# Other tables for the filling of the attention units, and sums of parts ahead of the low parts

## The reference, cut to what matters

```
proj = rmsnorm(x) @ w_in            # q_d k_d v_d  q_n k_n v_n  gate_b gate_c h_in
y_dil = dilated_attention(rope(q_d), rope(k_d), v_d)
y_na  = neighbourhood_attention(q_n, k_n, v_n, rpb)
y_conv = gate_b * conv3(gate_c * h_in)
x = x + rmsnorm(concat(y_dil, y_na, y_conv) @ w_out)
x = x + rmsnorm((silu(hf @ w_gate) * (hf @ w_up)) @ w_down)
```

## Time and profile before

| | us |
|---|---|
| median of 3 runs | 3051.28 |
| lowest, highest | 3050.6, 3051.84 |
| the profiled execution | 3046.58 |
| its span, first to last instruction | 3044.7 |
| TensorE busy in it | 2987.1 |
| VectorE busy | 2002.5 |
| ScalarE busy | 1242.8 |
| GpSimd busy | 937.6 |
| granted TensorE clock, mean | 0.998 |

### The profile page before, as it was taken

One profiled execution on the slowest core, in us unless ns is written; L12 is line 12 of the kernel. 1 busy time (PEld: TensorE's weight loads), 2 busy tenths in 40 slices (PEclk: granted clock), 3 DMA queues, 4 the chain that ended last, 5 costly groups with the idle time before them and its releaser, 6 DMA issues.

```text
span 3044.7 us, 50957 instructions
## 1 busy us (share of the span) xinstructions
PE 2987.1 (98%) x19620; PEld 2817.0 (93%) x19620; DVE 2002.5 (66%) x3740; ACT 1242.8 (41%) x2405; POOL 937.6 (31%) x757
## 2 busy tenths in 40 slices
PE   9999999999999999999999999999999999999997
PEld 7888877899999999999988888879999999999997
DVE  6766756388744447677877666563887444486787
ACT  5433444544422224444554334344544222254342
POOL 1211111664542225101542112117656222260011
PEclk9999999999999999999999999999999999999999
DMA  4111011333322115544521110113332221257345
GB/s 155 44 58 52 22 39 42 109 110 104 110 68 68 68 68 195 203 146 153 186 102 44 51 55 15 46 49 115 104 110 93 85 72 68 70 182 252 98 141 193
DMA packets 151519, 300.31 MB, mean 99 GB/s; under 512 B 16240, under 2 KB 74224, under 8 KB 151024
## 3 DMA queue, kind: packets, MB, share of 16 engines
q1 hardware_dynamic: 148976, 289.18, 28.5%
q10 hardware_dynamic: 2304, 7.87, 0.6%
HBM read 231.45 MB, written 57.67 MB: 95 GB/s over the span
## 4 chain that ended last, share of the span: by engine, by line
PE 87%; DVE 6%; issue 2%; POOL 1%; ACT 1%; DMA 1%; SPq 0%; POOLq 0%; DVEq 0%; ACTq 0%
PE PS L2606 26%; PE PS L2608 25%; PE PS L2607 25%; PE PS L2758 4%; PE PS L2727 4%; PE PS L2742 3%; PE PS L2644 1%; DVE PT L2334 1%; POOL OSS L1205 1%; DVE ACCUM L1938 1%; PE PS L2702 0%; ACT PT L1531 0%; DMA EYE<-small 0%; DVE ACCUM L1936 0%; DVE YB L2321 0%
## 5 line engine op out<-in xcount | busy, mean ns | idle before, releaser
L2606 PE MATMUL PS<-XH,WH 128*128 128x512 f32 (+1 forms) x1152 | 432.3, 375 | 14.6 <-DVE Rv L2208 4.1
L2608 PE MATMUL PS<-XH,WL 128*128 128x512 f32 (+1 forms) x1152 | 409.4, 355 | 0.0
L2607 PE MATMUL PS<-XL,WH 128*128 128x512 f32 (+1 forms) x1152 | 408.1, 354 | 0.0
L1227 POOL TENSOR_TENSOR GL<-GR,GH 128x512 fp32r<-128x512 f32 x186 | 252.1, 1367 | 366.4 <-ACT GH L1574 299.9
L2606 PE MATMUL PS<-DHH,DWH 128*128 128x384 f32 (+1 forms) x1056 | 328.5, 311 | 0.6 <-DVE ACCUM L2168 0.6
L2608 PE MATMUL PS<-DHH,DWL 128*128 128x384 f32 (+1 forms) x1056 | 326.6, 309 | 0.0
L2607 PE MATMUL PS<-DHL,DWH 128*128 128x384 f32 (+1 forms) x1056 | 325.8, 309 | 0.0
L2606 PEld LDWEIGHTS PS<-XH,WH 128*128 128x128 f32 x1152 | 217.0, 188 | 71.3 <-issue 19.6
L2334 DVE TENSOR_TENSOR PT<-PS,PT 128x512 fp32r<-128x512 f32 (+1 forms) x328 | 165.6, 538 | 165.3 <-ACT PT L1531 162.7
L2608 PEld LDWEIGHTS PS<-XH,WL 128*128 128x128 f32 x1152 | 217.1, 188 | 32.7
L1531 ACT ACTIVATE PT<-PS 128x512 fp32r<-128x512 f32 (+1 forms) x328 | 142.9, 477 | 247.2 <-PE PS L2742 242.8
(11 more groups left out here) (243 smaller groups left out, 8318.1 us busy)
## 6 DMA issues: line engine op xcount, KB each, us to landing
GR<-w_gu SPq DMA_DIRECT2D x62, 768.0 KB, 4.1
RAW<-w_in SPq DMA_DIRECT2D x48, 512.0 KB, 3.4
DHR<-hidden SPq DMA_DIRECT2D x66, 320.0 KB, 4.4
DWR<-w_down SPq DMA_DIRECT2D x66, 256.0 KB, 3.9
S3B<-w_down SPq DMA_DIRECT2D x66, 256.0 KB, 3.1
GR<-w_gu SPq DMA_DIRECT2D x62, 256.0 KB, 2.5
T3B<-hidden SPq DMA_DIRECT2D x44, 320.0 KB, 3.8
hidden<-S1T SPq DMA_DIRECT2D x44, 192.0 KB, 1.9
```

Of the source, the lines that this page charges most:

```text
L1227: nc.gpsimd.tensor_tensor(GL[v % 2][:, m, :, :], GR[v % 2][:, m, :, :], GH[v % 2][:, m, :, :].bitcast(F32), ALU.subtract).then_inc(s_wlo_r ...
L2606: nc.tensor.matmul(out, wh, xh, start=first, stop=False, skip_group_check=reopened)
L2607: nc.tensor.matmul(out, wh, xl, start=False, stop=False, skip_group_check=reopened)
L2608: return nc.tensor.matmul(out, wl, xh, start=False, stop=last, skip_group_check=reopened)
```

## The change

- `FILL_TILES` replaces `FILL_WIDTH`: the number of tiles of each step is written out. In blocks 0 and 1 a group still takes 4 + 4 tiles, the short one all 8 in one unit; in blocks 2 and 3 the nine groups take 19 units (the first group 2, 3, 3; the short one of k and q 2, 6); in block 4 the six groups take all 20 units.
- `SHORT_FIRST`: in four of the column tiles the short chunk is made first: order 2, 0, 1. With 4 + 4, 4 + 4 and 8 this sets at which units groups end.
- `ROPE_AT`: ropes stand in a table by unit, instead of one unit behind the group.
- SyncE's swaps follow the new order, and the load of ("q", 2) moves ahead of the last swap of ("q", 1).
- Taps: units 3, 5, 7 instead of 0, 1, 2 in block 2; 7, 8, 9 instead of 9, 10, 11 in block 4. GpSimd's scalings follow.
- `add_parts` stands ahead of the low parts of its unit instead of behind.
- At the start of block 4 the three bias operations stand behind the first drain and the split of v.

```diff
-FILL_FROM = (0, 0, 1, 1, 1)
-FILL_WIDTH = ((2, 2, 1) * 4, (2, 2, 1) * 4, (2,) * 9, (2,) * 9, (3,) * 6)
+FILL_FROM = (0, 0, 1, 1, 0)
+SHORT_FIRST = {("k", 1), ("v", 1), ("q", 2), ("c", 1)}
+EVEN, LATE, WHOLE, SLOW = (4, 4), (2, 6), (8,), (2, 3, 3)
...
+              ((2, 3, 3), (3, 1, 4), LATE, (1, 3, 1, 3), (1, 3, 1, 3), (2, 2, 2, 2)))
+ROPE_AT = ({7: ("k", 1, 2), 9: ("k", 1, 0), 11: ("k", 1, 1), 13: ("q", 1, 0), 15: ("q", 1, 1), 17: ("q", 1, 2)},
+           {3: ("k", 2, 0), 5: ("k", 2, 1), 6: ("k", 2, 2), 8: ("q", 2, 2), 9: ("q", 2, 0), 11: ("q", 2, 1)}, {}, {}, {})
+def chunks_in_turn(unit):
+    return (2, 0, 1) if unit in SHORT_FIRST else (0, 1, 2)
+def last_chunk(unit):
+    return chunks_in_turn(unit)[-1]
 def fill_steps(L, b):
     steps = [(None, 0, 0)] * FILL_FROM[b]
-    for group, width in zip(fill_groups(L, b), FILL_WIDTH[b]):
-        cuts = [KT * n // width for n in range(width + 1)]
-        steps += [(group, cuts[n], cuts[n + 1]) for n in range(width)]
+    for group, counts in zip(fill_groups(L, b), FILL_TILES[b]):
+        assert sum(counts) == KT
+        steps += [(group, sum(counts[:n]), sum(counts[:n + 1])) for n in range(len(counts))]
...
                 load((L, "k", 2))
-                for c in range(NCH):
+                for c in range(2):
                     swap(L, "q", 1, c)
                 load((L, "q", 2))
+                swap(L, "q", 1, 2)
...
-                        if (b, u) in ((0, 7), (2, 2), (4, 11)):
+                        if (b, u) in ((0, 7), (2, 7), (4, 9)):
                             scale_taps(L, b // 2)
...
                         y(u // 2 - 1)
+                    if u and u % 2 == 0:
+                        add_parts(u // 2 - 1)
                     for g, (a, n) in enumerate(quads(units[u][3])):
...
-                    if u and u % 2 == 0:
-                        add_parts(u // 2 - 1)
...
+                    drain(*cover[0])
+                    split_v(nb, slice(0, 4))
                     if b == LAST:
                         masked_biases(L, 1, 0)
                         masked_biases(L, 1, 1)
                         inner_biases(L, 1)
-                    drain(*cover[0])
-                    split_v(nb, slice(0, 4))
...
-                        if u and steps[u - 1][2] == KT and steps[u - 1][0] in ROPE:
-                            rope(*steps[u - 1][0])
+                        if u in ROPE_AT[b]:
+                            rope(L, *ROPE_AT[b][u])
...
-                        if b == 2 and u < 3:
-                            tap(L, 1, u)
+                        if b == 2 and u in (3, 5, 7):
+                            tap(L, 1, u // 2 - 1)
...
-                        if b == LAST and 9 <= u < 12:
-                            tap(L, 2, u - 9)
+                        if b == LAST and 7 <= u < 10:
+                            tap(L, 2, u - 7)
```

More of the change, by code:

```diff
@@ L168 @@
         (("h", 2), ("b", 2)))
-FILL_FROM = (0, 0, 1, 1, 1)
-FILL_WIDTH = ((2, 2, 1) * 4, (2, 2, 1) * 4, (2,) * 9, (2,) * 9, (3,) * 6)
+FILL_FROM = (0, 0, 1, 1, 0)
+SHORT_FIRST = {("k", 1), ("v", 1), ("q", 2), ("c", 1)}
+EVEN, LATE, WHOLE, SLOW = (4, 4), (2, 6), (8,), (2, 3, 3)
+FILL_TILES = ((EVEN, EVEN, WHOLE, WHOLE, EVEN, EVEN) * 2, (EVEN, EVEN, WHOLE, WHOLE, EVEN, EVEN) * 2,
+              (SLOW, EVEN, LATE, EVEN, EVEN, LATE, EVEN, EVEN, EVEN), (SLOW, EVEN, LATE, EVEN, EVEN, LATE, EVEN, EVEN, EVEN),
+              ((2, 3, 3), (3, 1, 4), LATE, (1, 3, 1, 3), (1, 3, 1, 3), (2, 2, 2, 2)))
[5 more added lines that the diff above has]
+    return chunks_in_turn(unit)[-1]
 def fill_groups(L, b):
-    return [(L, kind, i, c) for kind, i in FILL[b] for c in range(NCH)]
+    return [(L, kind, i, c) for kind, i in FILL[b] for c in chunks_in_turn((kind, i))]
 def cover_groups(L, b):
@@ L689, in final @@
             L, kind, i = unit
-            return GROUP[unit + (NOC - 1 if kind == "o" else 2,)]
+            return GROUP[unit + (NOC - 1 if kind == "o" else last_chunk((kind, i)),)]
         def gcol(L, which, k):
@@ L1038, in biases @@
                 if j == 0:
-                    sp.wait_ge(s_rope, ROPE[L, "q", 2, 2])
+                    sp.wait_ge(s_rope, ROPE[L, "q", 2, last_chunk(("q", 2))])
                     sp.dma_start(CMASK[:, :], tables[:, 2 * T + NLOG:]).then_inc(s_bias_in, 16)
@@ L1072, in _ @@
                 load((L, "b", 0))
-                for c in range(NCH):
+                for c in chunks_in_turn(("k", 1)):
                     swap(L, "k", 1, c)
                 load((L, "k", 2))
-                for c in range(NCH):
+                for c in range(2):
                     swap(L, "q", 1, c)
                 load((L, "q", 2))
+                swap(L, "q", 1, 2)
                 load((L, "v", 2))
@@ L1085, in _ @@
                 load((L, "h", 1))
-                for c in range(NCH):
+                for c in chunks_in_turn(("q", 2)):
                     swap(L, "q", 2, c)
@@ L2781, in fill @@
                     tiles(key, range(t0, t1))
-                drained((L, "v", b, 2))
+                drained((L, "v", b, last_chunk(("v", b))))
                 turn_v(nb, slice(0, 4))
```

## The result

The changed kernel takes 3019.07 us (median of four runs, 3017.97 to 3020.45), the kernel before 3051.56 beside it: a ratio of 0.9892, 95% interval 0.9881 to 0.9904. That is 32.5 us faster; 25.4 was forecast. A second series of the changed kernel gave 3019.43 (0.9894, 0.9875 to 0.9912).

The account below looks back on a forecast made before the run. TensorE, busy 2987.1 of 3044.7 us, was taken as the bound; only its attention stops could go. Per layer 22.2 falls to 2.0 + 2.6 + 2.8 + 2.1 = 9.5, 25.4 for two layers: 3026 us, range 3015 to 3040.

Parts of the forecast that it names:

- The ceiling of 22.2: TensorE's stops in a layer's attention blocks, 14.0 us idle plus about 0.2 for each of some 45: the most to win.
- A: Fill steps that open a group and wait for the last group's drain: 25 places, 10.5 us a layer falling to 2.0.
- B: Values that wait for the low parts of odd units: 12 places, 7.1 us a layer falling to 2.6.
- C: Transposes, `spread_recip` and one scores that wait for VectorE: 9 places, 4.6 us a layer falling to 2.8.
- The ports: Moved ropes and a tap on VectorE meet GpSimd's low parts of weights at shared SBUF ports: 2.1 us a layer lost.
- At no cost: Block 4's biases behind the first drain (scores' wait about 0.3, in C) and q's earlier load, said to move no wait.
- The sums: `add_parts` ahead of low parts: `spread_recip` loses its wait, low parts come 0 to 0.4 us later; counted in C.
- Rival 1: The ports take it back: five meetings a layer cost 2.0 us each instead of 0.4, giving 3042; chance 0.15.
- Rival 3: Stops only move: the gain of A comes back in B and C, giving 3047 us; chance 0.07.
- Rival 4: Slower: sums hold up low parts, 0.83 us for each pair that pays; at 45 pairs 3063 us; chance 0.03.
- rival 2: More goes than counted: block 4's stops (4.7 a layer after) halve, ports cost nothing, 9 us more, 3017; chance 0.15.
- The signs: Checks: idle 14.0 to about 6 us, few drain waits, stretches 11 to 14 shorter, nothing outside moving over a microsecond.

Follow-up runs that it names:

- blocks01_back: The changed kernel with blocks 0 and 1 as before (old tables, chunk order and rope places), the sums still ahead: 3028.39 us, ratio 0.9916.
- lows_apart: The changed kernel with GpSimd's low parts of weights kept out of VectorE's ropes and taps by waits: layer 0's blocks 475.65 us, against 476.30.
- both sums kernels: The kernel before with only the sums moved ahead of the low parts, 3046.2 us; the changed kernel with the sums behind them again, 3032.78 us.
- ropes_later: The changed kernel with every rope of blocks 0 and 1 one unit later, tables and drains unchanged: 3042.21 us in one run.

## Where the prediction was right and where not

The time lies in the range, and the stops that went are those of the text; the gain was forecast 3.5 us a layer too small (12.7 against 16.2). Several terms were taken too large and one stop of 1.0 wasn't seen, and these misses partly cancel: that the miss isn't larger is luck. Step by step, start against start in the timeline of layer 0 of the changed kernel:

- **The ceiling of 22.2.** What is left after is about 7.3 a layer where 9.5 was forecast, so the counted stops fell by 14.9. The blocks gained 16.3: the other 1.4 are gaps of 0.1 and less behind each stop, that weren't counted. So 22.2 was no ceiling, but 1.4 or more below it.
- **A, 10.5 to 2.0.** Right. Unit 18 of blocks 0 to 3 keeps 0.34 each, exactly the estimate from the drain's length; unit 3 of block 4 has 0.58 for 0.45, and the short groups behind one another cost 0.06 where no port meeting falls on them. It is 2.0 in all, beside 0.4 that goes to the ports.
- **B, 7.1 to 2.6.** It is 1.8 without the ports and the load. The value that was most off is unit 9 of block 4, taken at 1.3: 0.74. TensorE and VectorE there:

```profile
526.37 0.39 PE L2625 MATMUL PS<-XH,WL 128*128 128x512 f32 x1
527.34 1.43 PE L2775 MATMUL PS<-PT,V 128*128 128x256 f32 x10 [0.58 <-DVE PT L2353]
```

```profile
524.21 1.54 DVE L2271 SCALAR_TENSOR_TENSOR TA<-TC,STAT,TA 128x1281 f32<-128x1281 f32 x1
525.67 0.60 DVE L2338 TENSOR_TENSOR YB<-PS,YS 64x128 f32<-64x128 f32 x2
526.31 0.89 DVE L2353 TENSOR_TENSOR PT<-PS,PT 128x512 fp32r<-128x512 f32 x2
```

  The order of tap, outputs and low parts is as forecast and ends at 527.20. But the tap starts already 0.21 behind the unit's transposes (524.00), and three tiles of fill keep TensorE until 526.6; I had let the tap start later. The forecast set out from the 0.74 that this order cost before, and left out that the sums ahead free VectorE for the tap: with the sums ahead alone, that stop (unit 11 there) is 0.23.
- **C, 4.6 to 2.8.** It is 1.9. Counted up to the next transposes, units 10, 12, 14, 16 and 18 of block 4 wait 0.14, nothing, 0.24, 0.15 and 0.91, for the 0.5, 0.1, 0.45, 0.35 and 1.0 forecast. (The 2.63 of the earlier trace rows holds for unit 16 alone; in unit 18 the two transposes were 2.51 apart.) Block 4 in all was the largest miss: 4.7 forecast, 3.25 found, and its length fell by 3.2 where 1.2 was forecast.
- **The ports, 2.1.** The meetings at the units 11 came as forecast and cost nothing instead of 0.55 each; a late rope at the end of an odd unit has the slack, since nobody waits for its product soon. The one in unit 3 of block 1 makes the drain two units on late (0.4, for 0.1 forecast), that of the tap in unit 6 of block 0 makes the values behind it late (0.2, for 0.4), and the one in unit 6 of block 1 (0.5) didn't take place: together 0.6 a layer. "SBUF — State Buffer" of the Trainium skill, section "SBUF: two separate sides", speaks of a lock held for a whole instruction; the 2.52 beside 2.38 agree, and so does the drain from PSUM that keeps its length. The rule says how long VectorE is blocked, not whether TensorE waits for what VectorE does next: that is where the prediction was 1.5 off.
- **At no cost.** Here a step failed. The queue of SyncE was looked at for q only; the load of `h` 1 behind a swap of `k` 2 waits for a moved rope, and costs 1.0. It is why block 1 gained 1.25 and no more. The earlier load of q itself is right: blocks01_back keeps it, and its block 0 takes 117.28 us as with the sums alone (117.24); beside the new tables it wasn't tried. And the biases' move is worth 1.2 a layer and not 0.3: with the units ahead shorter, VectorE reaches them before their transfer, and stands.
- **The sums.** Their own part was counted in C. What the prediction doesn't say is that the tables need them: without them 7.3 of the 16.2 a layer are lost. It had the after-state right (the chain of 2.0 in units 16 and 18 was worked out with the sums ahead), but it gives no price to the edit.
- **The rivals.** Rival 1 is out by lows_apart: all meetings together cost 0.6 a layer, not 10. Rival 3 is out: A's gain didn't come back in B and C, though without the sums ahead a good part of it would have. Rival 4 is out by both sums kernels. Of rival 2 two thirds came true: block 4's stops are 1.45 and the ports 1.5 lower than forecast, 2.95 of its 4.5 a layer. The load takes 1.0 of that back, the small gaps that weren't counted give 1.4.
- **The signs.** Idle time fell to 4.3 where about 6 was forecast. Drains and ropes show as told; unit 9 waits 0.74, not about a microsecond. The stretches shortened by 16, not 11 to 14, so by its own words the prediction was wrong there, on the fast side. What moved outside the blocks was more than a microsecond as well, but between executions of the same code.

## What to carry to other kernels

Two edits can be worth more together than the sum of both alone (here 16.2 a layer, against 2.4 and 8.9): cost each of them also without the other, above all where one shortens the time of TensorE behind which the other's chain is hidden. When work is moved on one engine, follow the queue of every transfer that waits for it to the next thing in that queue, and who needs that. And an instruction that another engine stretches is a cost only where something waits for its engine within the next units (here at two of five places); look for the place before giving it a price.

## What the runs showed of the hardware

After the 6.07 us in which TensorE stood still in ropes_later its granted clock fell to 0.50, the lower of its two levels (1.2 for 2.4 GHz), and it was back at 1.00 from 248 us on. The stretches, with the granted clock behind POOL:

```profile
235.00:241.40 6.40, 0.34 (x2) 0.02 (x1) 1.16 (x3) 2.73 (x5) 1.60 (x1) 0.93 0.31 93
241.40:244.00 2.60, 2.59 (x12) 2.60 (x13) 2.46 (x9) 0.00 (x0) 1.05 (x2) 0.50 0.03 6
244.00:248.00 4.00, 4.00 (x21) 3.13 (x20) 2.12 (x5) 2.17 (x5) 0.00 (x0) 0.59 0.13 33
248.00:252.00 4.00, 4.00 (x21) 3.38 (x22) 1.97 (x6) 0.48 (x1) 0.00 (x0) 1.00 0.00 0
```

The five values took 1.41 us instead of the 0.83 in the changed kernel. The stops of up to 1.1 us that the change removes left the clock alone (1.00 in all stretches of attention, before and after), so removing them gave their own length back and no more.
